# Two projections and the settling of a head pair, laid out anew among the attention maxima of one layer

## The reference, cut to what matters

```python
valid = (jnp.abs(qpos[:, None] - kpos[None, :]) <= W) & (kpos >= 0)[None, :] & (kpos < S)[None, :]
s_loc = jnp.einsum('bqkgd,bskd->bkgqs', qn, kn).astype(jnp.float32) * scale
s_loc = jnp.where(valid, s_loc, NEG)
s_ctx = jnp.einsum('bqkgd,bckd->bkgqc', qn, kc).astype(jnp.float32) * scale
p = _sink_probs([s_loc, s_ctx], sink).astype(v.dtype)
return (jnp.einsum('bkgqs,bskd->bqkgd', p[..., :span], vn)
        + jnp.einsum('bkgqc,bckd->bqkgd', p[..., span:span + L], vc))
...
y = jnp.concatenate([ya.reshape(B, S, -1), yb.reshape(B, S, -1)], axis=-1) * jax.nn.silu(g)
```

## Time and profile before

| | |
|---|---|
| Median of 3 runs | 4753.09 us (4727.15 to 4758.35) |
| Profiled execution, its own time | 4750.99 us |
| Its span in the trace | 4748.9 us |
| Mean granted TensorE clock | 0.882 |
| PE, DVE, ACT, POOL busy | 4016.2, 2289.9, 1444.5, 422.8 us |
| The four pairs of this attention | 2216 to 2590 us, of which PE is busy 307.15 us |

### The profile page before, as it was taken

How to read it: one execution, slowest core, us unless ns; L and a number is a source line. 1 busy time by engine, 2 the same in 40 slices (tenths; PEclk the granted TensorE clock), 3 DMA queues, 4 the chain that set the end, 5 groups by cost and what they waited for, 6 DMA issues and landing times. The chain is left out here.

```text
span 4748.9 us, 44428 instructions
## 1 busy us (share of the span) xinstructions
PE 4016.2 (85%) x18448; PEld 3137.0 (66%) x18448; DVE 2289.9 (48%) x3662; ACT 1444.5 (30%) x2369; POOL 422.8 (9%) x398
## 2 busy tenths in 40 slices
PE   4899987887979999987878888876978998788877
PEld 2688865656758888865666656654756776565556
DVE  4899246555542222345554444445444555334344
ACT  3221234343121111123443233333233434222231
POOL 2112100001010000001000222221010000000000
PEclk9899878897989999998888889877978988888888
DMA  2133230003401111121001000001200000000012
GB/s 76 58 108 131 98 112 24 18 18 111 147 31 49 45 49 40 54 76 36 20 20 33 15 15 14 19 15 70 84 30 26 22 26 14 28 5 8 8 50 92
DMA packets 67514, 225.23 MB, mean 47 GB/s; under 512 B 7848, under 2 KB 11944, under 8 KB 67312
## 3 DMA queue, kind: packets, MB, share of 16 engines
q1 hardware_dynamic: 43056, 132.68, 8.5%
q0 software_dynamic: 20800, 77.12, 4.5%
q10 hardware_dynamic: 3456, 12.58, 0.7%
HBM read 180.95 MB, written 37.74 MB: 46 GB/s over the span
## 5 line engine op out<-in xcount | busy, mean ns | idle before, releaser
L1924 PE MATMUL PS<-m,m 128*128 128x512 f32 (+4 forms) x4216 | 1758.6, 418 | 357.8 <-ACT m L2172 55.0
L1925 PE MATMUL PS<-m,m 128*128 128x512 f32 (+4 forms) x4216 | 1651.1, 392 | 0.0
L1926 PE MATMUL PS<-m,m 128*128 128x512 f32 (+4 forms) x4216 | 1648.8, 391 | 0.0
L1924 PEld LDWEIGHTS PS<-m,m 128*128 128x128 f32 (+1 forms) x4216 | 836.7, 199 | 745.2 <-issue 290.0
L1926 PEld LDWEIGHTS PS<-m,m 128*128 128x128 f32 (+1 forms) x4216 | 844.6, 201 | 158.8
L1925 PEld LDWEIGHTS PS<-m,m 128*128 128x128 f32 (+1 forms) x4216 | 847.9, 201 | 127.7 <-issue 2.9
L2520 DVE TENSOR_TENSOR m<-PS,m 128x512 fp32r<-128x512 f32 x352 | 240.5, 689 | 415.7 <-ACT m L2183 414.0
L2256 DVE TENSOR_TENSOR m<-m,m 128x1024 fp32r<-128x1024 f32 (+4 forms) x203 | 211.1, 1040 | 428.4 <-ACT m L2089 427.8
L2183 ACT CAST m<-PS 128x512 fp32r<-128x512 f32 x352 | 203.9, 585 | 365.5 <-PE PS L2011 365.1
L2011 PE MATMUL PS<-m,m 128*128 128x128 f32 x1408 | 252.6, 309 | 67.8 <-DVE m L2516 29.1
L2089 ACT CAST m<-m 128x1024 fp32r<-128x1024 f32 (+4 forms) x235 | 212.9, 906 | 249.9 <-PE PS L1926 188.7
(11 more groups left out here) (194 smaller groups left out, 3714.8 us busy)
## 6 DMA issues: line engine op xcount, KB each, us to landing
m<-in_w SPq DMA_DIRECT2D x220, 512.0 KB, 3.3
g_scratch<-m ACTq DMA_DIRECT2D x24, 512.0 KB, 2.8
m<-g_scratch POOLq DMA_DIRECT2D x24, 512.0 KB, 4.6
m<-in_w SPq DMA_DIRECT2D x32, 256.0 KB, 2.7
x_scratch<-m POOLq DMA_DIRECT2D x2, 4096.0 KB, 12.3
y_scratch<-m POOLq DMA_DIRECT2D x15, 512.0 KB, 2.9
m<-y_scratch POOLq DMA_DIRECT2D x15, 512.0 KB, 5.7
y_scratch<-m POOLq DMA_DIRECT2D x7, 640.0 KB, 3.3
```

Source lines behind the costliest of these rows:

```text
L1924: pe.e.engine.matmul(o, L[0], X[0], start=start, stop=False)
L1925: pe.e.engine.matmul(o, L[0], X[1], start=False, stop=False)
L1926: return pe.e.engine.matmul(o, L[1], X[0], start=False, stop=stop)
```

## The change

Five things change in the plan.

- The gate projection no longer stands alone. One generator gives the 24 q steps and then the 24 gate steps; two are pulled after a window's maxima and three after a context block's, and the rest is drained after `tops`.
- `turned` moves into a hook of the attention loop, which calls it after the second `cross` (and so, on VectorE, between the first and the second residue).
- `settle` is cut into four: the first product at once, and three pieces kept in a list, `later`: the reciprocal of the left half, that of the right half, and both last products.
- `piece()` takes one of them: after each residue of the loop and after each maximum. The next settling first takes all that are left, and so do the switch from q to gate steps and the end of the loop over pairs.
- The output of a pair is stored by a callback, when the last piece of its context chunk has been placed.

```diff
@@ Crossed
-    def settle(self, w, gate=None, gate_there=(), y=None, y_free=()):
+    def settle(self, w, gate=None, gate_there=(), y=None, y_free=(), then=None):
...
+        while self.later:
+            self.piece()
...
         self.u_free = [(self.S.outd, n)]
-        return (self.S.outd, n)
+        for i in range(2):
+            half = L[:, w // 2 * i:w // 2 * (i + 1)]
+            self.later.append(lambda i=i, half=half: self.p.add("settled", of=n, i=i, L=half, gate=gate))
+
+        def last():
+            self.p.add("times", of=n, U=U, L=L, gate=gate, y=y, y_free=list(y_free))
+            if then:
+                then((self.S.outd, n))
+        self.later.append(last)
+
+    def piece(self):
+        if self.later:
+            self.later.pop(0)()
@@ Crossed.run
                 if x:
                     self.rest(x)
+                    self.piece()
                 x = self.cross(segments, keys, queries, ext, sm, masks, after)
                 after = []
+                if hook:
+                    hook(i)
@@ for j in range(4)
+            nxt_t, q_steps = z_linear(f"eq{j + 1}" if j < 3 else "fq0", zq, 0.125, at.fill_banks)
+            zg_t, g_steps = z_linear(f"eg{j}", zg, 1.0, at.fill_banks)
+
+            def fill_steps():
+                p.add("ready", on="act", after=q_t)
+                yield from q_steps
+                while at.later:
+                    at.piece()
+                p.add("ready", on="act", after=z_free)
+                yield from g_steps
+            fill = Fill(fill_steps(), 48)
...
                             q_t + k_t, m_t)
-                    q_fill.pull(2)
+                    fill.pull(2)
+                    at.piece()
                 if b % 2:
...
-                    q_fill.pull(2)
+                    fill.pull(3)
+                    at.piece()
...
-            q_fill.drain()
+            fill.drain()
...
-            g_fill = Fill(steps, 24)
-            g_fill.pull(8)
-            q_done = turned(zq, nxt_t)
-            g_fill.drain()
...
-                y_t.append(at.settle(w, zg[:, q0:q0 + w], zg_t))
+                at.settle(w, zg[:, q0:q0 + w], zg_t, then=y_t.append if q0 < T else finished)
+
+            def finished(event, j=j, y_t=y_t):
+                z_free[:] = [y_store(j, zg, TC, y_t + [event])]
+
+            def hook(i):
+                if i == 1:
+                    q_done[:] = turned(zq, nxt_t)
@@ vector_program
-            e.reciprocal(L, L).then_inc(*dve.says(S.norm, (n, "recip")))
-            dve.wait_ge(S.norm, (n, "recip"))
+        elif s.kind == "settled":
+            if s["gate"] is not None:
+                dve.wait_ge(S.norm, (s["of"], "gate"))
+            e.reciprocal(s["L"], s["L"]).then_inc(*dve.says(S.norm, (s["of"], "recip", s["i"])))
+        elif s.kind == "times":
+            U, L, of = s["U"], s["L"], s["of"]
+            dve.wait_ge(S.norm, (of, "recip", 1))
+            if s["gate"] is not None:
+                e.tensor_tensor(U, U, L, ALU.mult).then_inc(*dve.says(S.norm, (of, "y")))
+                dve.wait_ge(S.norm, (of, "y"))
+                e.tensor_tensor(s["gate"], s["gate"], U, ALU.mult).then_inc(*dve.says(S.outd, of))
```

More of the change, by code:

```diff
@@ L549, in __init__ @@
         self.nr = self.nx = 0
-        self.waiting = []
+        self.later = []
         self.last_pv = None
@@ L646, in gather @@
         self.last_pv = (self.S.pv, ("x", x["n"]))
-    def settle(self, w, gate=None, gate_there=(), y=None, y_free=()):
+    def settle(self, w, gate=None, gate_there=(), y=None, y_free=(), then=None):
+        assert gate is None or gate_there
         n = self.p.id()
@@ L654, in settle @@
                  (L[0:64, :], o[0][64:128, :]), (L[64:128, :], o[1][0:64, :])]
+        while self.later:
+            self.piece()
         self.p.add("settle", n=n, parts=parts, after=self.last_pv, u_free=self.u_free, gate=gate, gate_there=list(gate_there),
-                   t=G, U=U, L=L, y=y, y_free=list(y_free))
+                   t=G, U=U, L=L)
         for b in self.o_banks:
@@ L659, in settle, with run @@
         self.u_free = [(self.S.outd, n)]
-        return (self.S.outd, n)
-    def run(self, chunks, keys, queries, ext, sm, values, after, v_after, fill=None, extra=None, settled=None, end=None):
+        for i in range(2):
[9 more added lines that the diff above has]
+            self.later.pop(0)()
+    def run(self, chunks, keys, queries, ext, sm, values, after, v_after, fill=None, extra=None, settled=None, hook=None, end=None):
         total = sum(len(steps) for _, _, steps in chunks)
@@ L666, in run @@
         behind = []
+        i = 0
         def one_behind():
@@ L676, in run @@
         for q0, w, steps in chunks:
-            for i, (segments, masks) in enumerate(steps):
+            for k, (segments, masks) in enumerate(steps):
                 if x:
                     self.rest(x)
+                    self.piece()
                 x = self.cross(segments, keys, queries, ext, sm, masks, after)
                 after = []
-                n = -(-fill.left // total) if fill else 0
-                total -= 1
+                if hook:
+                    hook(i)
+                n = -(-fill.left // (total - i)) if fill else 0
+                i += 1
                 if fill:
                     fill.pull(n // 2)
-                behind.append((x, q0, w, i == 0, i == len(steps) - 1))
+                behind.append((x, q0, w, k == 0, k == len(steps) - 1))
                 if len(behind) > 2:
@@ L1491, in schedule @@
         chunks = [(q0, w, [(seg, masked(seg)) for seg in steps]) for q0, w, steps in window_steps]
-        z_free = []
+        z_free, q_done = list(tok_t), []
         ext_free = []
         for j in range(4):
-            nxt_t, steps = z_linear(f"eq{j + 1}", zq, 0.125, at.fill_banks) if j < 3 else z_linear("fq0", zq, 0.125, at.fill_banks)
-            p.add("ready", on="act", after=q_t)
-            q_fill = Fill(steps, 24)
+            nxt_t, q_steps = z_linear(f"eq{j + 1}" if j < 3 else "fq0", zq, 0.125, at.fill_banks)
[8 more added lines that the diff above has]
+            fill = Fill(fill_steps(), 48)
             at.start()
@@ L1545, in schedule @@
                    lambda h, y: (vh[:, y, 64 * h:64 * h + 128], vl[:, y, 64 * h:64 * h + 128]),
-                   rows_t + made_t, tok_t + made_t, None, sinks, settled, end)
+                   rows_t + made_t, tok_t + made_t, None, sinks, settled, hook, end)
             at.stop()
             ext_free = [at.last_cross, at.last_pv]
-            z_free = [y_store(j, zg, TC, y_t)]
+        while at.later:
+            at.piece()
         fq_events = q_done
@@ L2570, in vector_program @@
             dve.wait_ge(S.evac, (n, 3))
-            L, U = s["L"], s["U"]
             if s["gate"] is not None:
                 dve.wait_ge(S.exp, (n, "gate"))
-                e.scalar_tensor_tensor(out=L, in0=s["t"], scalar=1.0, in1=L, op0=ALU.add,
+                e.scalar_tensor_tensor(out=s["L"], in0=s["t"], scalar=1.0, in1=s["L"], op0=ALU.add,
                                        op1=ALU.mult).then_inc(*dve.says(S.norm, (n, "gate")))
-                dve.wait_ge(S.norm, (n, "gate"))
-            e.reciprocal(L, L).then_inc(*dve.says(S.norm, (n, "recip")))
-            dve.wait_ge(S.norm, (n, "recip"))
+        elif s.kind == "settled":
             if s["gate"] is not None:
-                e.tensor_tensor(U, U, L, ALU.mult).then_inc(*dve.says(S.norm, (n, "y")))
-                dve.wait_ge(S.norm, (n, "y"))
-                e.tensor_tensor(s["gate"], s["gate"], U, ALU.mult).then_inc(*dve.says(S.outd, n))
+                dve.wait_ge(S.norm, (s["of"], "gate"))
[7 more added lines that the diff above has]
+                e.tensor_tensor(s["gate"], s["gate"], U, ALU.mult).then_inc(*dve.says(S.outd, of))
             else:
@@ L2585, in vector_program @@
                     dve.wait_ge(*ev)
-                e.tensor_tensor(s["y"], U, L, ALU.mult).then_inc(*dve.says(S.outd, n))
+                e.tensor_tensor(s["y"], U, L, ALU.mult).then_inc(*dve.says(S.outd, of))
         elif s.kind == "turned":
```

## The result

The changed kernel takes 4694.89 us in the median of 4 runs (4689.84 to 4699.28). The kernel before took 4742.95 in the 4 runs of that comparison, and the ratio is 0.9909 (95% interval 0.9885 to 0.9932). Later, six further runs of it beside eleven of the kernel before gave 0.9926 (0.9902 to 0.9949). So the change is worth some 0.7 to 0.9%, near 40 us, where 24 had been forecast. It is 34 us under 4729: 10 of them are that the kernel before came out 10 lower than in its first runs, near 14 are a gain in the four pairs that is larger than forecast (37.6 for 24.0), and the other 10 are how medians of a few runs differ.

A forecast was written before the change was run, and what follows sets the result against it. The bound was taken to be TensorE, interrupted by a VectorE queue served in the wrong order. Terms -6.8 -4.8 -9.8 -9.0 -7.4 +0.3 +8.2 +5.3 summed to -24.0 us, from 4753.1 to 4729 (chance 0.58); range 4707 to 4756.

The forecast's parts named there:

- A: Gate projection steps moved into the maxima, before these are turned: -6.8 us of waits, -4.8 of clock for three pairs.
- B: Settling of chunk 0 in pieces between residues: -9.8 us of TensorE's waits for residues, -9.0 of clock behind them.
- C: End of a pair: context chunk's reciprocal and products go behind the next pair's first maxima; -7.4 us, no clock counted.
- D: Rotation moved behind the first residue, making the second late: +8.2 us of waits, +5.3 if the gap halves the clock.
- last: The last pair pays 0.15 us for the pieces and some semaphores: +0.3 us.
- The clock goes by something else than these gaps: Rival, chance 0.20: across the four pairs only waits count, -15.5 us, 4738; 4743 if D's gap halves the clock nevertheless.
- The rotation hides: Rival, chance 0.11: D's +8.2 and +5.3 fall away; with B's larger clock loss of 11.6, -40 us, 4713.
- Slower: Rival, chance 0.04: D's gap leaves the array at half clock until chunk 0 is settled; +13 us, 4766.
- waits only change their name: Rival, chance 0.07: evacuations by ScalarE and of the context chunk hold TensorE instead; B and C nothing, +2.2 us, 4755.

## Why the prediction was wrong

The mechanism was right and so was the sign; the size was not. Each step against the two profiles, waits first, then the rest of the term, which is clock in A, B and C:

| Step | Forecast | Measured waits | Measured rest | Measured |
|---|---|---|---|---|
| A, steps before the turn | -6.8 -4.8 | -8.4 | -4.8 | -13.2 |
| B, pieces of chunk 0 | -9.8 -9.0 | -8.9 | -11.8 | -20.7 |
| C, end of a pair | -7.4 +0 | -7.9 | -2.6 | -10.5 |
| D, rotation | +8.2 +5.3 | +5.8 | +1.1 | +6.9 |
| last | +0.3 | | | -0.1 |
| sum | -24.0 | -19.4 | -18.1 | -37.6 |

(B and D are stretches of their own. A and C share the stretch from the first maximum to the first `cross`, 23.7 us shorter in all; their waits are told apart by the rows, A's clock is the 1.6 of three pairs, and C's rest is what remains. In the second profiles of both kernels the same reckoning gives A -13.2, B -22.0, C -10.6 and D +6.9, with 1.0 and not 2.6 as C's rest.)

The step that failed is D's clock term. Its last sentence, "if this new gap halves the clock as often as the likes of it do", gave +5.3, and the granted clock behind the new gap was 1.00 in all four pairs: nothing of it came. That is 5.3 of the 13.6 us by which the sum was off. The likes were waits of 1.9 to 3.3 us, and the new one turned out to be 1.44. Behind 1.44 no half clock came in any of 20 pairs (five profiles with that wait), behind 2.05 in two of four, behind 2.78 in four of four, at this same place. The other 1.3 us of D are the wait, forecast at 2.05 a pair. The forecast counted it from the weight load, and by the weight loads it is 1.9 (7.5 in four, above); the matmuls issued ahead ran on for another 0.4, so TensorE idled 1.44. The stretch as a whole grew by 1.7 a pair, 6.9 in all, at full clock, so the +1.1 in the table is not clock.

C's sentence "the array is likely to start at half clock ... as it does after 5.1, so no clock is counted" failed next: 2.6 us came back in these two profiles, 1.0 in the second ones. B's price was 1.9 too small. I took the nearer of two readings of the clock's cost, 8.8 (written as 9.0), where the carried-on line had said 11.6. In the changed kernel the 70 matmuls of the earlier trace rows take 8.1 us at a granted 1.00, between the two readings of 7.8 and 8.5, so what they had lost was 10.5; the table's 11.8 has another 1.5 of half clock behind the evacuation's wait in it, three pairs before and two after, which B does not touch. Its waits came to 8.9 for the 9.8 forecast. A's remaining gap of 0.4 did not appear; TensorE reached the turn just as VectorE was through. Two slips of the sum cancel: D's wait, by its own times, is 2.0 a pair and not 2.05, and 1.6 x 0.85 x 4 is 5.4 and not 5.3. The rows of the maxima, put at 8.3 us behind the turn, came at 7.3 in three pairs.

The rule weighed in the prediction (the Trainium skill, "TensorE: Matmul & The Clock Gate", section "HAM oscillation — how this bites in real kernels") would make idleness of this length free of charge. The runs do not agree: 2.05 us cost 3.0 us of clock in two pairs of four, and the waits that the change removed took half clock along too, that of 2.1 us in three of four pairs, those of 1.9 to 3.3 in four of four. The measurement decides. That 1.44 us was free agrees with it.

The rivals. "The clock goes by something else than these gaps" is half right: half clock follows the gaps, but which pair it strikes is not explained. "The rotation hides" did not come: the rotation cost 6.9. That its -40 is the nearest of all to -37.6 is luck: it had left out a wait that did come, and clock in B and C made up for it. "Slower" and "waits only change their name" are refuted; the evacuation, named there, stood at 18.2 to 18.3 throughout and took over nothing. The range was too narrow for another reason too: its lower end lay 6 us under that rival's 4713, while the rest of the program alone moved by 50 between single executions.

Open: what lets half clock strike one pair and spare another with the same wait. Over the thirteen profiles it followed 0 of 20 waits of 1.44 us, 21 of 52 of 1.75 (the evacuation of chunk 0), 11 of 16 of 2.1 (the turn) and 29 of 39 of 2.9 (the evacuation of chunk 1, pairs 0 to 2), but 12 of 12 behind the settling in one go, five of which were 1.9 and the others 3.3 to 3.4. So longer waits take it along more often, and length alone does not decide; no run varies what TensorE does before or behind such a wait.

## What to carry to other kernels

Where TensorE is the bound, price a wait as its length plus the clock that it is likely to take along, and count both ways: half of this gain was matmuls running at 2.4 instead of 1.2 GHz. Count the half clock only where no wait for another engine follows it; ahead of such a wait it was free here (7.1 + 2.5 against 5.6 + 4.0). A long operation on a helper engine is best cut and put behind what TensorE needs next, which brought 31 of the 38 us; spreading the matmuls alone brought nothing that whole runs could show. When a step is moved, look for the place where its engine idles for as long as it lasts: the rotation cost 1.7 us a pair behind the first residue and none four steps later.

## What the runs showed of the hardware that was not expected

- The same stretch of work with the same wait of 2.05 us took 23.6 or 26.7 us, by whether half clock followed. Four pairs of one execution showed both, twice each.
- A single further 0.6 us on VectorE (1.44 to 2.05 us of waiting) was enough for this to begin, by that one execution.
- Half clock ahead of a wait made that wait shorter by just what it had cost: 30 matmuls took 7.1 or 5.6 us, the wait behind them 2.5 or 4.0, and the sum stayed 9.6.
- Untouched stages differed between executions by up to 50 us (4335.7 to 4386.1), more than the change is worth, while the stage that was changed repeated within 0.3 us before (373.4, 373.1) and 1.3 after (335.8, 334.6). A profile of one stage told more than several whole runs.
